# Delta rule: sums of squares from two rounded parts, with query sums and value transposes ahead of the output sums

## What is computed

```python
def l2_norm(x):
    xf = x.astype(jnp.float32)
    return xf * lax.rsqrt(jnp.sum(xf * xf, axis=-1, keepdims=True) + EPS)
...
    q = l2_norm(q.reshape(B, S, DN_HEADS, DN_HEAD_DIM)) * (DN_HEAD_DIM ** -0.5)
    k = l2_norm(k.reshape(B, S, DN_HEADS, DN_HEAD_DIM))
...
    o = gated_delta_rule(q, k, v, g, beta)
    o = rms_norm(o, out_norm) * jax.nn.silu(z...)
...
    # gated_delta_rule, the loop over chunks
    def step(state, inp):
        qd, kd, u_c, w_c, a_c, gl = inp
        v_new = u_c - jnp.einsum('bhcd,bhde->bhce', w_c, state)
        o = jnp.einsum('bhcd,bhde->bhce', qd, state) + jnp.einsum('bhcs,bhse->bhce', a_c, v_new)
        state = state * gl[..., None, None] + jnp.einsum('bhcd,bhce->bhde', kd, v_new)
        return state, o
```

## Time and profile before

| | |
|---|---|
| runs, median of 3 | 1583.88 us (1583.28 to 1585.54) |
| profiled execution | 1580.38 us |
| its span, first to last instruction | 1577.5 us |
| PE busy | 1534.2 us, 97% |
| DVE / ACT / POOL busy | 595.1 / 603.7 / 560.0 us |
| granted TensorE clock, mean | 0.997 of full speed |

### The profile page before, as it was taken

The page is one execution under the profiler, slowest core; times in us unless marked ns, Lnnn a source line. Parts: engine busy times, 40 slices in busy tenths (PEclk is TensorE's granted clock), DMA queues, the critical chain, the costliest instruction groups (busy, mean ns, idle before and its releaser), DMA issues.

```text
span 1577.5 us, 21190 instructions
## 1 busy us (share of the span) xinstructions
PE 1534.2 (97%) x7900; PEld 1267.5 (80%) x7900; DVE 595.1 (38%) x996; ACT 603.7 (38%) x998; POOL 560.0 (36%) x270
## 2 busy tenths in 40 slices
PE   6889999999999999999999999999999999999998
PEld 6868888888887778888888887777688888888887
DVE  3355556565565422221022224566432222012210
ACT  5643444334442533322232234576433332223221
POOL 4522321323212244434533444221234444444442
PEclk9999999999999999999999999999999999999999
DMA  7411111111110133233323233111123332433322
GB/s 250 125 64 54 41 30 51 54 41 44 38 34 11 50 94 113 88 98 92 117 81 106 82 85 124 48 41 33 36 78 107 109 94 76 124 94 94 90 84 80
DMA packets 39218, 124.41 MB, mean 79 GB/s; under 512 B 4192, under 2 KB 5472, under 8 KB 39136
## 3 DMA queue, kind: packets, MB, share of 16 engines
q1 hardware_dynamic: 38976, 123.01, 25.5%
q10 hardware_dynamic: 160, 0.26, 0.1%
HBM read 120.89 MB, written 2.10 MB: 78 GB/s over the span
## 4 chain that ended last, share of the span: by engine, by line
PE 93%; DVE 3%; ACT 3%; issue 1%; DMA 0%; POOL 0%; SPq 0%; DVEq 0%; ACTq 0%
PE bank L564 72%; PE bank L730 3%; PE bank L717 3%; PE bank L728 2%; ACT ws L1091 2%; PE bank L1025 1%; DVE act_lo L1536 1%; PE bank L892 1%; PE bank L851 1%; DVE ws L1539 1%; PE bank L576 1%; PE bank L1049 1%; PE bank L738 1%; PE bank L881 1%; PE bank L764 1%
## 5 line engine op out<-in xcount | busy, mean ns | idle before, releaser
L511 POOL TENSOR_TENSOR w_lo<-w_raw,w_hi 128x1024 fp32r<-128x1024 f32 (+1 forms) x250 | 539.9, 2175 | 835.3 <-ACT w_hi L1091 835.1
L564 PE MATMUL bank<-act_hi,w_hi 128*128 128x512 f32 (+1 forms) x1776 | 708.3, 399 | 6.7 <-DVE act_lo L1536 2.7
L564 PE MATMUL bank<-act_hi,w_lo 128*128 128x512 f32 (+1 forms) x1776 | 680.1, 383 | 0.0
L564 PE MATMUL bank<-act_lo,w_hi 128*128 128x512 f32 (+1 forms) x1776 | 679.5, 383 | 0.0
L564 PEld LDWEIGHTS bank<-act_hi,w_hi 128*128 128x128 f32 x1776 | 335.4, 189 | 74.7 <-issue 13.5
L564 PEld LDWEIGHTS bank<-act_hi,w_lo 128*128 128x128 f32 x1776 | 334.7, 188 | 65.8
L564 PEld LDWEIGHTS bank<-act_lo,w_hi 128*128 128x128 f32 x1776 | 335.5, 189 | 62.2 <-issue 5.6
L1091 ACT ACTIVATE w_hi<-w_raw 128x1024 fp32r<-128x1024 f32 (+1 forms) x250 | 230.5, 953 | 88.8 <-PE bank L564 86.6
L1530 DVE TENSOR_TENSOR ws<-bank,ws 128x512 f32<-128x512 f32 x110 | 75.9, 690 | 336.2 <-PE bank L564 326.2
L1091 ACT ACTIVATE ws<-ws 128x512 f32<-128x512 f32 (+2 forms) x135 | 87.1, 647 | 154.6 <-DVE ws L1530 107.4
L1798 DVE TENSOR_TENSOR xT<-xT,bank 128x512 f32<-128x512 f32 (+1 forms) x48 | 33.0, 687 | 257.0 <-PE bank L564 257.0
(11 more groups left out here) (150 smaller groups left out, 1218.7 us busy)
## 6 DMA issues: line engine op xcount, KB each, us to landing
w_raw<-w_stream SPq DMA_DIRECT2D x154, 512.0 KB, 3.6
w_raw<-w_out SPq DMA_DIRECT2D x32, 384.0 KB, 3.1
w_raw<-w_down SPq DMA_DIRECT2D x32, 384.0 KB, 3.1
w_raw<-w_down SPq DMA_DIRECT2D x32, 320.0 KB, 3.2
ws<-x_in SPq DMA_DIRECT2D x1, 2048.0 KB, 8.8
ws<-mem_in SPq DMA_DIRECT2D x2, 512.0 KB, 4.7
out<-ws SPq DMA_DIRECT2D x1, 1024.0 KB, 4.2
sq_c<-squares_in SPq DMA_DIRECT2D x1, 768.0 KB, 7.1
```

Of the source, the lines that this page charges most:

```text
L511: nc.gpsimd.tensor_tensor(w_lo[:, s, 0:width * P], w_raw[:, s, 0:width * P], w_hi[:, s, 0:width * P].bitcast(F32), ALU.subtract).then_inc( ...
L564: mm = nc.tensor.matmul(acc, wt[:, c % RING, wsl], at[:, act0(k0 + k), off:off + n], start=(start and k == 0 and m == 0), stop=(stop and k ...
```

## The change

The three sums of squares of a head become two one-pass products each: ones by the rounded square, plus ones by the rest of it.

- ACT squares into the PSUM bank of the sums, then copies it, rounded, into tile 23 of `act_hi` (key and query share it, `SUM_T`) or tile 16 of `act_lo` (output). DVE subtracts the rounded part from PSUM and leaves the rest in `act_lo` (`split_k`, `split_q`, `split_o`). PE multiplies a rounded matrix of ones by both parts (`two_part_sums`).
- The key and query share a tile, so the query's rounded copy waits for the key sums' products (`ss_done`).
- PE: the next head's key sums move from state step 3 to step 2, the piece of step 2 to step 3. The next head's query sums and value transposes come ahead of the output sums. Two pieces of the first projection tile come ahead of the row products, and one more of them between the key transposes and the key products.
- ACT: `square_q` moves from behind the output's square to ahead of `silu_v`.
- DVE: `split_k` stands behind the state's update of step 1; at step 2 the third tap of the value tile moves behind the state's update; `split_q` and `split_o` stand behind the last copy of new values.
- At the start ACT makes the rounded ones.

```diff
+            def two_part_sums(acc, upper_, lower_):
+                nc.tensor.matmul(psum(acc), ones_r, upper_, start=True, stop=False)
+                return nc.tensor.matmul(psum(acc), ones_r, lower_, start=False, stop=True)
             def key_sums_dn(h):
                 pe.wait_ge(S.sq_done, 2 * h + 1)
-                nc.tensor.matmul(psum(D[1]), sq(ONES), w(PM), start=True, stop=True).then_inc(S.ss_done, 1)
+                two_part_sums(D[1], act_hi[:, SUM_T, :], act_lo[:, SUM_T, :]).then_inc(S.ss_done, 1)
+            def query_sums_dn(h):
                 pe.wait_ge(S.sq_done, 2 * h + 2)
+                two_part_sums(D[0], act_hi[:, SUM_T, :], act_lo[:, SUM_T, :]).then_inc(S.ss_done, 1)
+            def delta(h, fill):
+                if h == 0:
+                    pe.wait_ge(S.pick_done, 1)
+                    key_sums_dn(0)
+                    query_sums_dn(0)
+                    value_transposes(0)
+                fill(0, 2)
...
-                fill(0, 2)
                 pe.wait_ge(S.kn_done, h + 1)
...
                 transposes4(D[5], KN).then_inc(S.ktr_done, 1)
+                fill(2, 3)
...
-                        if t < NT - 1:
-                            fill(23 + 2 * t, 24 + 2 * t)
+                        if t != 2:
+                            fill(24 + t, 25 + t) if t == 1 else fill(27, 28)
                         elif h + 1 < DN_HEADS:
                             key_sums_dn(h + 1)
...
                 fill(30, 32)
-                pe.wait_ge(S.osq, h + 1)
-                nc.tensor.matmul(psum(D[2]), sq(ONES), w(E1), start=True, stop=True).then_inc(S.oss, 1)
+                if h + 1 < DN_HEADS:
+                    query_sums_dn(h + 1)
+                    value_transposes(h + 1)
+                pe.wait_ge(S.osq_lo, h + 1)
+                two_part_sums(D[2], act_lo[:, OHI_T, :], act_lo[:, OLO_T, :]).then_inc(S.oss, 1)
...
             def square_q(h):
                 if due(h):
-                    act.wait_ge(S.o_done, h)
-                a(w(E0), w(CQ), ACT.Square).then_inc(S.sq_done, 1)
+                    act.wait_ge(S.at_done, h)
+                a(psum(D[0]), w(CQ), ACT.Square).then_inc(S.sq_hi, 1)
+                act.wait_ge(S.sq_hi, 4 * h + 3)
+                act.wait_ge(S.ss_done, 2 * h + 1)
+                a(act_hi[:, SUM_T, :], psum(D[0]), ACT.Copy).then_inc(S.sq_hi, 1)
...
                 if following:
+                    square_q(h + 1)
                     silu_v(h + 1)
                 act.preload_act_table_set("natural_log_exp_and_others")
                 act.wait_ge(S.o_done, h + 1)
-                a(w(E1), psum(D[5]), ACT.Square).then_inc(S.osq, 1)
+                a(psum(D[2]), psum(D[5]), ACT.Square).then_inc(S.osq, 1)
+                act.wait_ge(S.osq, 2 * h + 1)
+                a(act_lo[:, OHI_T, :], psum(D[2]), ACT.Copy).then_inc(S.osq, 1)
                 if following:
-                    square_q(h + 1)
                     rr_k(h + 1)
...
+            def split_k(h):
+                dve.wait_ge(S.sq_hi, 4 * h + 2)
+                sub(act_lo[:, SUM_T, :], psum(D[1]), hi(SUM_T)).then_inc(S.sq_done, 1)
...
-                    fill(2, t + 1)
+                    if t < 2 or not following:
+                        fill(2, t + 1)
...
                         stt(state[:], state[:], dn(GL)[:, h, t:t + 1], bank[:, D[4], 0:P], ALU.mult, ALU.add
                             ).then_inc(S.s_done, 1)
+                    if following and t == 1:
+                        split_k(h + 1)
+                    if following and t == 2:
+                        fill(2, t + 1)
+                if following:
+                    split_q(h + 1)
+                split_o(h)
                 fill(3)
```

More of the change, by code:

```diff
@@ L201, in yoco_kernel @@
             sz_done = sem("sz_done")
+            sq_hi = sem("sq_hi")
             sq_done = sem("sq_done")
@@ L242, in yoco_kernel @@
             osq = sem("osq")
+            osq_lo = sem("osq_lo")
             oss = sem("oss")
@@ L416, in rows @@
             return act_hi[P // 2 * half:P // 2 * (half + 1), 18, :]
+        SUM_T, OHI_T, OLO_T = KT + CAT - 1, 16, 17
+        ones_r = act_lo[:, 18, 0:P]
         def row_cols(half):
@@ L659, in half_tiles, with value_transposes @@
                 return range(NT // 2 * g, NT // 2 * (g + 1))
+            def two_part_sums(acc, upper_, lower_):
+                nc.tensor.matmul(psum(acc), ones_r, upper_, start=True, stop=False)
+                return nc.tensor.matmul(psum(acc), ones_r, lower_, start=False, stop=True)
             def key_sums_dn(h):
                 pe.wait_ge(S.sq_done, 2 * h + 1)
-                nc.tensor.matmul(psum(D[1]), sq(ONES), w(PM), start=True, stop=True).then_inc(S.ss_done, 1)
-            def delta(h, fill):
-                if h == 0:
-                    key_sums_dn(0)
+                two_part_sums(D[1], act_hi[:, SUM_T, :], act_lo[:, SUM_T, :]).then_inc(S.ss_done, 1)
+            def query_sums_dn(h):
                 pe.wait_ge(S.sq_done, 2 * h + 2)
-                if due(h):
-                    pe.wait_ge(S.at_done, h)
-                nc.tensor.matmul(psum(D[0]), sq(ONES), w(E0), start=True, stop=True).then_inc(S.ss_done, 1)
+                two_part_sums(D[0], act_hi[:, SUM_T, :], act_lo[:, SUM_T, :]).then_inc(S.ss_done, 1)
+            def value_transposes(h):
                 pe.wait_ge(S.c_ready, 2 * h + 2)
@@ L678, in delta @@
                 transposes4(D[4], CV).then_inc(S.vtr_done, 1)
+            def delta(h, fill):
[5 more added lines that the diff above has]
+                fill(0, 2)
                 if h == 0:
                     pe.wait_ge(S.rw_done, 2)
-                    pe.wait_ge(S.pick_done, 1)
+                    pe.wait_ge(S.pick_done, 2)
                 if due(h):
@@ L698, in delta @@
                 mm.then_inc(S.gg_done, 1)
-                fill(2, 9)
+                fill(3, 9)
                 pe.wait_ge(S.z_done, h + 1)
@@ L1224, in square_k @@
                     act.wait_ge(S.tz_mm, 12 * h)
-                a(w(PM), w(CK), ACT.Square).then_inc(S.sq_done, 1)
+                a(psum(D[1]), w(CK), ACT.Square).then_inc(S.sq_hi, 1)
+                act.wait_ge(S.sq_hi, 4 * h + 1)
+                if due(h):
+                    act.wait_ge(S.ss_done, 2 * h)
+                a(act_hi[:, SUM_T, :], psum(D[1]), ACT.Copy).then_inc(S.sq_hi, 1)
             def square_q(h):
                 if due(h):
-                    act.wait_ge(S.o_done, h)
-                a(w(E0), w(CQ), ACT.Square).then_inc(S.sq_done, 1)
+                    act.wait_ge(S.at_done, h)
[3 more added lines that the diff above has]
+                a(act_hi[:, SUM_T, :], psum(D[0]), ACT.Copy).then_inc(S.sq_hi, 1)
             def rr_k(h):
@@ L1289, in _ @@
             conv_tile(0, 1)
+            a(ones_r, sq(ONES), ACT.Copy).then_inc(S.pick_done, 1)
             a(act_hi[:, 16:18, :].rearrange("p a (b c) -> p (a b) c", c=P),
@@ L1648, in normed_k, with split_q, split_o @@
                 mul(w(KN), w(CK), psum(D[1])).then_inc(S.kn_done, 1)
+            def split_k(h):
+                dve.wait_ge(S.sq_hi, 4 * h + 2)
+                sub(act_lo[:, SUM_T, :], psum(D[1]), hi(SUM_T)).then_inc(S.sq_done, 1)
+            def split_q(h):
+                dve.wait_ge(S.sq_hi, 4 * h + 4)
+                sub(act_lo[:, SUM_T, :], psum(D[0]), hi(SUM_T)).then_inc(S.sq_done, 1)
+            def split_o(h):
+                dve.wait_ge(S.osq, 2 * h + 2)
+                if due(h):
+                    dve.wait_ge(S.oss, h)
+                sub(act_lo[:, OLO_T, :], psum(D[2]), act_lo[:, OHI_T, :].bitcast(F32)).then_inc(S.osq_lo, 1)
             def o_finish(h):
@@ L1717, in delta @@
                             ).then_inc(S.s_done, 1)
+                    if following and t == 1:
[5 more added lines that the diff above has]
+                split_o(h)
                 fill(3)
-                dve.wait_ge(S.osq, h + 1)
+                dve.wait_ge(S.osq, 2 * h + 1)
                 dve.wait_ge(S.sz_done, h + 1)
@@ L1731, in _ @@
             conv_tile(0, 3)
+            split_k(0)
+            split_q(0)
             normed_k(0)
```

## The result

The changed kernel takes 1595.05 us (median of 4, 1593.85 to 1595.59) against 1583.58 of before (four executions; the table of before has three of them): ratio 1.0072, 95% interval 1.0054 to 1.0089. It is slower by about 11.5 us. The prediction said slower, 1588.1 us, with a range up to 1591; the time lies above it.

A forecast was written before the change was run, and what follows sets the result against it. PE's own list of work was taken to bound the delta rule's heads. Head 0 +1.84, seven turns +1.40 and last head +0.97 gave +4.2 us on the median 1583.9: 1588.1 us, slower, range 1582.5 to 1591.

The forecast's parts named there:

- PE's list bounds the heads, a rounded pass is 0.23 us, a sum saves 0.40.: Delta rule's heads: PE's work sets the time; two 0.23 us passes replace a 0.86 us product; 24 sums would give 9.6 us.
- The key sums wait 0.87 us for a subtraction behind the state's update.: Seven turns, key sums: asked for a step earlier, PE stands 0.87 us for DVE's subtraction; state steps end 0.57 us late.
- The output sums wait 0.54 us, since tap, silu and table load are late.: Seven turns, output sums: ACT's square starts 0.60 us late behind the table load, so PE stands for 0.54 us.
- rivals A and B: All turns: A, both waits hidden, 1578.3 us, chance 0.10; B, only the first wait holds, 1585.1 us, chance 0.17.
- A turn costs +0.20.: Each turn between heads: 1.2 us saved is paid back in two waits and two restarts; seven turns +1.4 us.
- The table load has no drain.: ACT's table load at the turns: 1.28 us without drain; by the skill's page the square would start 1.38 us later.
- Head 0 costs +1.84, the last head +0.97.: First and last head: square, copy and subtraction make PE wait with nothing to cover it, +1.84 and +0.97 us.
- The rest of the program is untouched.: Stretches ahead of head 0's sums and behind the last head's passes: predicted difference 0.
- Base.: Starting point of the forecast: the runs' median of 1583.88 us, 3.5 above the profiled execution's 1580.38.
- Rival C: Solve at each turn: DVE reaches L1533 some 2 us later, PE waits 1.0 a turn, +7, 1595 us; chance 0.08.

The follow-up runs named there:

- the run with both DVE instructions moved: Changed kernel with key subtraction behind the state's copy of step 0 and third tap ahead of the update of step 2: 1580.83 us, ratio 0.9990.
- the busy filling: Changed kernel with five plain products that nobody reads put into PE's two waits at head 0, sums still in two parts: 1590.05 us, ratio 1.0043.
- the long wait in the old kernel: Kernel before with four ACT squares that nobody reads ahead of head 0's key square, so PE stands longer: 1587.68 us, ratio 1.0032.

## Why the prediction was wrong

- *PE's list bounds the heads, a rounded pass is 0.23 us, a sum saves 0.40.* Right: 0.23 in the trace, and a turn without waits is 1.24 us shorter, by the run with both DVE instructions moved.
- *The key sums wait 0.87 us for a subtraction behind the state's update.* Right to the hundredth; moving that subtraction took the wait away.
- *The output sums wait 0.54 us, since tap, silu and table load are late.* Right in mechanism, 0.48 in size; putting the tap back took it away. By rivals A and B the waits would have been hidden; the rows show both.
- *A turn costs +0.20.* The period shows +0.30 (49.18 less 48.88), the seven turns +1.77 instead of +1.40. In the chain the transposes right behind the row products take 0.58 us, and I had copied 0.44; as the wait is 0.06 shorter than worked out, this accounts for the 0.10 only roughly.
- *The table load has no drain.* Right: 224.04 + 1.28, then the square at 225.33. The Trainium skill's 1380 ns of drain ("ScalarE: Activation LUTs", What ACT_TABLE_LOAD costs) did not show here.
- *Head 0 costs +1.84, the last head +0.97.* This is the step that failed: it put the clock behind these waits at full speed without a reason. The waits were right: from ACT's square to the key sums are 2.10 us at head 0 (122.09 to 124.19; 2.02 predicted), and at the last head ACT's square to the end of the sums takes 2.73 us (510.23 to 512.96) instead of 1.77 (500.96 to 501.61 + 1.12), +0.96. But both steps priced the products behind the wait by rows taken at 2.4 GHz. Behind them the clock was at 1.2 GHz: an estimated 2.8 us more at head 0 and 1.6 at the last head (1.41 - 0.86 for L862, 6.55 - 5.47 for the passes). At head 0 the busy filling and the long wait in the old kernel show the cause from both sides; at the last head it rests on the traces compared above. The Trainium skill ("TensorE: Matmul & The Clock Gate", What's actually happening) says that the low clock is the default and that activity releases it. These traces agree: behind PE's idle time the granted clock was 0.51, and with PE at work again it was back at 1.00 from 131 us on. I had not asked what a standing PE does next.
- *The rest of the program is untouched.* True of the code. In time, the changed kernel lost a further 1.4 to 2.6 us behind the last head's passes. That stretch, with the same work in all kernels, takes 1068.4 to 1069.7 us in the three traces with the old sums and 1066.7 to 1071.3 in the ten others, and differs by stretches at 1.2 GHz (the granted clock is 0.91 from 981 to 1001 us in the changed kernel and 1.00 at the same work, 969 to 989 us, in before). Whether the change makes them more frequent is open.
- *Base.* The first profile lay 3.5 us under the median, and its repetition came out at the median; starting from the median was right.
- *Rival C, a wait carried into the solve, 1595 us.* That it names the measured time is chance: behind the output sums' wait the chain after has only PE's products up to the solve (from 227.32 to past 239 us), so its mechanism is absent.

Terms and sizes: predicted 1.84 + 1.40 + 0.97 = 4.2; measured in the same three stretches 4.60 + 1.77 + 2.59 = 8.96, of which some 4.4 are the clock. These alone would have moved the forecast from 1588.1 to 1592.5, out of its range. The median's difference is 10.6 to 11.5; the 1.6 to 2.5 us beyond 8.96 stay open.

## What to carry to other kernels

A cheaper product pays only if its operands come as early as the old ones did: each new operation on another engine has to be put where that engine stands idle, and one place in its list can be worth more than all savings. Price a new wait of TensorE twice, once for the wait and once for what may run behind it at half the clock; at places with nothing to fill in (first and last turn of a loop), keep the older, longer form. Read a change of a few microseconds by stretches between two rows of the chain: those agreed within 0.1 us between executions whose totals differed by 4.

## What the runs showed of the hardware

- Behind an idle time of PE of 2.23 us at head 0 the clock fell to 1.2 GHz in 6 of 6 traces, within some 0.4 us of PE's next product and ahead of the second idle time of 1.47 us; behind one of 0.82 us at the same place it did not, in both traces of before. Behind one of 2.89 us it did (one trace). Behind 2.03 us at the last head it fell in 5 of 7 traces, behind 0.69 us in none of six.
- Two executions of one program differ by whole stretches at 1.2 GHz: 55 to 75 us at 1.00 in one and 0.83 in the other; the work up to L793 ended at 113.42 us in the one and at 116.55 in the other.
- An ACT instruction started 0.01 us behind the end of a table load (224.04 + 1.28, then 225.33).
